# Normalising two attentions after the value product instead of before it, in a fused two-block transformer kernel

## The reference

```python
def causal_block_attention(q, k, v):          # 8 heads, q and k 96 wide, v 64 wide
    sc = jnp.einsum('bhqd,bhkd->bhqk', qi, kf) * scale
    sc = jnp.where(key_idx[None, :] <= q_idx[:, None], sc, -jnp.inf)
    p = jax.nn.softmax(sc, axis=-1)
    return jnp.einsum('bhqk,bhkd->bqhd', p, vf)
...
h = h + jnp.concatenate([o_gla, o_mla], axis=-1) @ w_out      # gated linear attention, then the above
hn = rms_norm_2(h, norm_xa)
xq = rms_norm_2((hn @ xa_w_q).reshape(b, s, 4, 128), xa_q_norm)
p = jax.nn.softmax(xq . xk * 128 ** -0.5)                     # cross attention, 4 heads of 128, 256 keys
h = h + (p @ xv).reshape(b, s, 512) @ xa_w_o
```

## Time and profile before

| | |
|---|---|
| executions | 971.32, 969.14, 969.3 us, median 969.3 |
| the profiled execution | 971.32 us, span of its records 969.6 us |
| PE / PEld busy | 960.1 us (99%) / 943.8 us (97%) |
| DVE / ACT / POOL busy | 689.9 us (71%) / 535.2 us (55%) / 123.3 us (13%) |
| chain that ended last | PE 96%, DVE 2%, DMA 1%, ACT 1% |
| granted PE clock | full in all 40 slices |

### The profile page before, as it was taken

How to read it: one execution, slowest core, us unless ns; L and a number is a source line. 1 busy time by engine, 2 the same in 40 slices (tenths; PEclk the granted TensorE clock), 3 DMA queues, 4 the chain that set the end, 5 groups by cost and what they waited for, 6 DMA issues and landing times.

```text
span 969.6 us, 20487 instructions
## 1 busy us (share of the span) xinstructions
PE 960.1 (99%) x8286; PEld 943.8 (97%) x8286; DVE 689.9 (71%) x1081; ACT 535.2 (55%) x775; POOL 123.3 (13%) x81
## 2 busy tenths in 40 slices
PE   7999999999999999999999999999999999999998
PEld 7999999999999999999999999989999999999998
DVE  4766766467869968877767655687697688788752
ACT  6545455345658964465544465477565665455531
POOL 0211110000026100002111102300001022223100
PEclk9999999999999999999999999999999999999999
DMA  7776575555454454575666674245245355665761
GB/s 245 217 214 204 185 239 180 182 152 185 150 199 153 135 170 135 173 258 178 209 187 206 206 233 154 88 143 173 87 140 172 125 174 163 193 207 173 251 208 63
DMA packets 169086, 172.37 MB, mean 178 GB/s; under 512 B 5684, under 2 KB 166974, under 8 KB 168894
## 3 DMA queue, kind: packets, MB, share of 16 engines
q1 hardware_dynamic: 169006, 171.45, 55.5%
q10 hardware_dynamic: 16, 0.00, 0.0%
HBM read 170.39 MB, written 1.06 MB: 177 GB/s over the span
## 4 chain that ended last, share of the span: by engine, by line
PE 96%; DVE 2%; DMA 1%; ACT 1%; issue 0%; SPq 0%; DVEq 0%
PE acc L730 86%; PE part L776 1%; PE acc L776 1%; DMA xraw<-in_x 1%; PE part L816 1%; PE part L840 1%; DVE wl L474 1%; PE part L1124 1%; PE part L826 1%; DVE al L1906 0%; PE part L860 0%; PE part L1114 0%; PE part L1320 0%; PE part L1301 0%; PE part L1147 0%; PE part L939 0%
## 5 line engine op out<-in xcount | busy, mean ns | idle before, releaser
L455 ACT ACTIVATE wh<-raw 128x1024 fp32r<-128x1024 f32 (+2 forms) x292 | 317.2, 1111 | 270.5 <-PE acc L730 122.7
L474 DVE TENSOR_TENSOR wl<-raw,wh 128x1024 fp32r<-128x1024 f32 (+3 forms) x294 | 391.1, 1370 | 54.0 <-ACT wh L455 52.2
L730 PE MATMUL acc<-ah,wh 128*128 128x256 f32 x1520 | 424.7, 279 | 0.7 <-DVE al L1906 0.3
L730 PE MATMUL acc<-al,wh 128*128 128x256 f32 x1520 | 420.8, 277 | 0.0
L730 PE MATMUL acc<-ah,wl 128*128 128x256 f32 x1520 | 420.7, 277 | 0.0
L730 PEld LDWEIGHTS acc<-ah,wh 128*128 128x128 f32 x1520 | 285.3, 188 | 4.7 <-issue 3.6
L730 PEld LDWEIGHTS acc<-al,wh 128*128 128x128 f32 x1520 | 285.4, 188 | 0.1
L730 PEld LDWEIGHTS acc<-ah,wl 128*128 128x128 f32 x1520 | 285.4, 188 | 0.0
L2769 POOL TENSOR_TENSOR sil<-sil,rstd 128x512 f32<-128x512 f32 x33 | 61.5, 1863 | 307.6 <-ACT sil L1427 215.5
L730 PE MATMUL acc<-hh,wh 128*128 128x256 f32 x352 | 97.4, 277 | 0.0
L730 PE MATMUL acc<-hh,wl 128*128 128x256 f32 x352 | 97.3, 276 | 0.0
(11 more groups left out here) (444 smaller groups left out, 1525.6 us busy)
## 6 DMA issues: line engine op xcount, KB each, us to landing
raw<-in_ffn_w_up SPq DMA_DIRECT2D x33, 1024.0 KB, 5.3
raw<-in_ffn_w_down SPq DMA_DIRECT2D x24, 1408.0 KB, 6.3
raw<-in_w_in SPq DMA_DIRECT2D x33, 1024.0 KB, 5.3
raw<-in_ffn_w_gate SPq DMA_DIRECT2D x32, 1024.0 KB, 5.3
raw<-in_w_out SPq DMA_DIRECT2D x8, 1024.0 KB, 4.9
raw<-in_w_proj_attn SPq DMA_DIRECT2D x4, 1024.0 KB, 4.9
raw<-in_w_proj_mlstm SPq DMA_DIRECT2D x4, 1024.0 KB, 5.6
raw<-in_xa_w_kv SPq DMA_DIRECT2D x4, 1024.0 KB, 4.9
```

Of the source, the lines that this page charges most:

```text
L455: nc.scalar.activation(wh[:, slot, a * nw:b * nw], raw[:, slot, a * nw:b * nw], ACT.Copy).then_inc(S("w_hi"), 1)
L474: nc.vector.tensor_tensor(wl[:, slot, a * nw:b * nw], raw[:, slot, a * nw:b * nw], f(wh[:, slot, a * nw:b * nw]), SUB).then_inc(S("w_lo"), 1)
L730: ins = mm(dst, a, b, start=st and q == 0, stop=en_ and q == 2, skip_group_check=True)
```

## The change

The division by the row sum moves behind the value product in both attentions. `ml_divided` and `xa_divided` go, so the transposes wait for the exponentials. In `ml_outputs` and `xa_outputs` the operands change places: the transposed probabilities are the weights and the values move, 64 columns in the causal attention and 128 in the cross attention. The result is token by feature. DVE takes it out with a multiplication by the reciprocal of the sum into `ytok`, and four extra groups of four PE transposes (`lo_T` twice, `xo_T` twice) bring it back to feature by token. The first two slabs of `wo2` are multiplied in the order first half, transposes, first half of the next slab, second half, second half of the next, and steps of ACT and DVE are placed anew.

```diff
@@ PE
             def ml_transposes(u):
-                pe.wait_ge(*signal("ml_pn", u + 1))
+                pe.wait_ge(*signal("ml_ex", 4 * u + 4))
...
-                for pair in range(2):
+                for h in range(4):
+                    c = (4 * g + h) * 64
                     for b in range(blk + 1):
-                        for odd in range(2):
-                            h = 2 * pair + odd
-                            c = (4 * g + h) * 64
-                            ins = mm(Q[4][64 * odd:64 * odd + 64, pair * P:(pair + 1) * P], vm[:, b, c:c + 64],
-                                     probT2[:, b, h * P:(h + 1) * P], start=pair + b == 0, stop=b == blk, skip_group_check=True)
+                        ins = mm(Q[4][:, h * 64:(h + 1) * 64], probT2[:, b, h * P:(h + 1) * P], vm[:, b, c:c + 64],
+                                 start=h + b == 0, stop=b == blk, skip_group_check=True)
                 ins.then_inc(S("ml_pv"), 1)
...
             s, n = SLAB0["wo2"], ACC0["wo2"]
             open_acc(n)
-            product(s, 0, 8, n, ah, al, before=mixer_operand, narrow=(1, Q[0]))
+            product(s, 0, 8, n, ah, al, before=mixer_operand, part=0, used=(1, 1))
+            pe.wait_ge(*signal("ml_yo", 4))
+            pe.wait_ge(*signal("ml_pt", 4))
+            for j in (2, 3):
+                y_transposes(j, Q[j - 2], "lo_T")
             open_acc(n + 1)
-            product(s + 1, 0, 8, n + 1, ah, al)
+            product(s + 1, 0, 8, n + 1, ah, al, part=0, used=(0, 0), narrow=(1, Q[4]))
+            product(s, 0, 8, n, ah, al, before=mixer_operand, part=1, used=(1, 1))
+            product(s + 1, 0, 8, n + 1, ah, al, part=1, used=(0, 2))
...
-                pe.wait_ge(*signal("xa_pn", u + 1))
+                pe.wait_ge(*signal("xa_ex", 4 * u + 4))
...
-                        ins = mm(Q[pair][:, c * T + u * P:c * T + (u + 1) * P], xv[:, b, h * P:(h + 1) * P],
-                                 (probT2, probT3)[u][:, b, h * P:(h + 1) * P], start=u + c + b == 0, stop=b == 1, skip_group_check=True)
+                        ins = mm(Q[pair][:, u * 256 + c * P:u * 256 + (c + 1) * P], (probT2, probT3)[u][:, b, h * P:(h + 1) * P],
+                                 xv[:, b, h * P:(h + 1) * P], start=u + c + b == 0, stop=b == 1, skip_group_check=True)
...
+            def xo_transposes(pair):
+                pe.wait_ge(*signal("xa_yo", pair + 1))
+                for c in range(2):
+                    for b in range(TB):
+                        h, o = 2 * pair + c, (c * TB + b) * P
+                        ins = nc.tensor.transpose(Q[2 + pair][:, o:o + P], ytok[:, b, h * P:(h + 1) * P], ident)
+                ins.then_inc(S("xo_T"), 1)
...
-            product(s + 1, 0, 8, n + 1, mo, mlo, tokens=True, before=at((3, lambda: xa_transposes(0)), (4, lambda: xa_transposes(1)), (6, lambda: xa_outputs(0, 0)), (6, lambda: xa_outputs(1, 0))))
+            product(s + 1, 0, 8, n + 1, mo, mlo, tokens=True, before=at((0, lambda: xa_transposes(0)), (4, lambda: xa_transposes(1)), (6, lambda: xa_outputs(0, 0)), (6, lambda: xa_outputs(1, 0))))
+            xo_transposes(0)
+            xa_outputs(0, 1)
+            xa_outputs(1, 1)
...
                     if (part, k) == (0, 0):
-                        xa_outputs(0, 1)
-                        xa_outputs(1, 1)
+                        xo_transposes(1)
@@ ACT
-                    act.wait_ge(*signal("ml_yo", 2 * j - 2))
-                    ins = A_(ah[:, 2 * j:2 * j + 2, :], yl[:, j - 2, :, :], ACT.Copy)
+                    act.wait_ge(*signal("lo_T", j - 1))
+                    ins = A_(pairs(ah, j), Q[j - 2][:, :], ACT.Copy)
...
             split_hi(act, s)
+            ml_transposed(3)
             y_hi(0)
             y_hi(1)
-            ml_transposed(3)
-            y_hi(2)
-            y_hi(3)
             split_hi(act, s + 1)
             xk_squares(0)
             xk_squares(1)
+            y_hi(2)
+            y_hi(3)
...
-            split_hi(act, s + 4, only=0)
             xa_transposed(0)
...
+            split_hi(act, s + 4)
             xa_transposed(1)
-            split_hi(act, s + 4, only=1)
+            token_out("xv", 1, lambda b: xv[:, b, 256:512], ms7[:, 2:4])
             for j in range(2):
-                act.wait_ge(*signal("xa_pv", j + 1))
-                A_(pairs(mh, j), Q[j][:, :], ACT.Copy).then_inc(S("xo_hi"), 1)
+                act.wait_ge(*signal("xo_T", j + 1))
+                A_(pairs(mh, j), Q[2 + j][:, :], ACT.Copy).then_inc(S("xo_hi"), 1)
                 if j == 0:
-                    token_out("xv", 1, lambda b: xv[:, b, 256:512], ms7[:, 2:4])
                     split_hi(act, SLAB0["xo"] + 1)
@@ DVE
             def ml_leave(u):
+                dve.wait_ge(*signal("ml_ex", 4 * u + 4))
+                link(V.reciprocal(rin[:, u % 2, :], rsm[:, u % 2, :]))
                 dve.wait_ge(*signal("ml_pv", u + 1))
-                V.tensor_copy(yl[:, g, :, blk * P:(blk + 1) * P], two_t(Q[4][:, 0:256])).then_inc(S("ml_yo"), 1)
+                V.tensor_tensor(by_head(ytok[:, blk, 512 + 256 * g:768 + 256 * g], 4), by_head(Q[4][:, 0:256], 4),
+                                across(rin[:, u % 2, :], 64), MUL).then_inc(S("ml_yo"), 1)
...
             xk_out(1)
             ml_leave(3)
+            split_lo(dve, SLAB0["wo2"] + 1)
             y_lo(2)
             y_lo(3)
-            split_lo(dve, SLAB0["wo2"] + 1)
...
+            def xa_leave(pair):
+                if pair == 0:
+                    dve.wait_ge(*signal("xa_ex", 8))
+                    link(V.reciprocal(rin[:, :, :], rsm[:, :, :]))
+                dve.wait_ge(*signal("xa_pv", pair + 1))
+                for u in range(2):
+                    ins = V.tensor_tensor(by_head(ytok[:, u, pair * 256:(pair + 1) * 256], 2), by_head(Q[pair][:, u * 256:(u + 1) * 256], 2),
+                                          across(rin[:, u, 2 * pair:2 * pair + 2], P), MUL)
+                ins.then_inc(S("xa_yo"), 1)
...
+            xa_leave(0)
             xo_low(0)
             split_lo(dve, s + 1, only=0)
+            xa_leave(1)
+            split_lo(dve, s + 1, only=1)
             xo_low(1)
-            split_lo(dve, s + 1, only=1)
```

More of the change, by code:

```diff
@@ L96, in shared_signals @@
         "mixer2_pe": [("mem_ps", 4), ("kv_ps", 1), ("uk_ps", 3), ("gl_z", 1), ("uq_ps", 3), ("kq_T", 8),
-                      ("gl_keT", 1), ("gl_att", 1), ("gl_dS", 3), ("gl_o", 2), ("go_T", 2), ("xq_ss", 2)],
+                      ("gl_keT", 1), ("gl_att", 1), ("gl_dS", 3), ("gl_o", 2), ("go_T", 2), ("lo_T", 2), ("xq_ss", 2),
+                      ("xo_T", 2)],
     }
@@ L349, in build @@
         xtok = ytok
-        yl = xn[:, :, :].rearrange("p c t -> p (c t)").rearrange("p (g f) -> p g f", g=2)[:, :, 512:1024]\
-            .rearrange("p g (c t) -> p g c t", c=2)
         qsq = xn[:, :, :].rearrange("p (j c) t -> p j (c t)", c=2)
@@ L2507, in ml_maxima, with ml_leave @@
                                            op0=ADD, op1=MIN, accum_out=rmx[:, u % 2, h:h + 1]).then_inc(S("ml_mx"), 1)
-            def ml_divided(u):
-                w = (u % 2 + 1) * P
+            def ml_leave(u):
+                g, blk = u // 2, u % 2
                 dve.wait_ge(*signal("ml_ex", 4 * u + 4))
                 link(V.reciprocal(rin[:, u % 2, :], rsm[:, u % 2, :]))
[L2514 to L2520, removed]
                 dve.wait_ge(*signal("ml_pv", u + 1))
-                V.tensor_copy(yl[:, g, :, blk * P:(blk + 1) * P], two_t(Q[4][:, 0:256])).then_inc(S("ml_yo"), 1)
+                V.tensor_tensor(by_head(ytok[:, blk, 512 + 256 * g:768 + 256 * g], 4), by_head(Q[4][:, 0:256], 4),
+                                across(rin[:, u % 2, :], 64), MUL).then_inc(S("ml_yo"), 1)
             def gl_masks():
@@ L2606, in y_lo @@
                 else:
-                    ins = V.tensor_tensor(al[:, 2 * j:2 * j + 2, :], yl[:, j - 2, :, :], f(ah[:, 2 * j:2 * j + 2, :]), SUB)
+                    ins = V.tensor_tensor(pairs(al, j), Q[j - 2][:, :], f(pairs(ah, j)), SUB)
                 ins.then_inc(S("y_lo"), 1)
@@ L2616, in _ @@
             split_lo(dve, g0 + 3)
-            ml_divided(0)
             slab_used(dve, g0 + 2)
@@ L2623, in _ @@
             gl_masks()
-            ml_divided(1)
             split_lo(dve, g0 + 5)
@@ L2630, in _ @@
             gl_state(2)
-            ml_divided(2)
             split_lo(dve, SLAB0["xk"])
@@ L2638, in _ @@
             gl_gated()
-            ml_divided(3)
             xk_out(0)
@@ L2712, in _ @@
             xa_maxima(1)
-            xa_divided(0)
-            xa_divided(1)
             split_lo(dve, s + 4)
@@ L2719, in xo_low @@
                 dve.wait_ge(*signal("xo_hi", j + 1))
-                V.tensor_tensor(pairs(ml, j), Q[j][:, :], f(pairs(mh, j)), SUB).then_inc(S("xo_lo"), 1)
+                V.tensor_tensor(pairs(ml, j), Q[2 + j][:, :], f(pairs(mh, j)), SUB).then_inc(S("xo_lo"), 1)
             def xo_added(k):
@@ L2810, in _ @@
             norm_pairs("n6")
```

(2 more changed lines are left out.)

## The result

The changed kernel takes 975.3 us (median of 6, 973.31 to 976.08), the kernel before 969.28 us in the same comparison. The ratio is 1.0052, 95% interval 1.0042 to 1.0062. In a second comparison, where the kernel before had a median of 970.95 us, the same changed kernel took 975.28 us, ratio 1.0038 (1.0021 to 1.0055). These ratios lie near those of the means over all executions (17 of the changed kernel in the first comparison, whose median is 974.79); the ratios of the medians are 1.0062 and 1.0045. The forecast was 973.7 us, 1.0045 times the median before, slower with a chance of 0.84.

What follows compares the result with a forecast made beforehand. PE, busy 99%, bounds the kernel, so added PE steps cost full length. Terms 1.28 - 0.15 + 0.79 + 0.20 + 0.63 + 1.62 = +4.4 us on a median of 969.3 give 973.7 us; range 971.0 to 976.5.

Steps and rivals of the forecast that it cites:

- the value product: Causal attention: 48 calls with 128 weight columns at 0.101 us each, 4.86 instead of 3.58 us, so +1.28 us.
- the cross attention: From the `xo` transposes on: 0.8 us of transposes, 0.1 of fresh starts, 0.7 more waiting, together +1.62 us.
- the third slab: In `wo2`, PE waits for DVE's late addition that empties the accumulator, plus a fresh start: +0.63 us.
- Divisions: DVE multiplications and reciprocals leave the chains to the transposes; PE gains -0.15 us, DVE loses some 5 us net.
- `lo_T`: Eight added PE transposes that bring the causal attention's result back to feature by token: +0.79 us.
- pace: `wo2` products in the new block order: more at 0.118 us before the narrow matmul, 11.32 against 11.12, +0.20 us.
- The wait for `xv`: Before `xa_outputs(0, 1)` in the cross attention, PE waits for ACT to write `xv`: 0.7 us.
- the wait of 0.25 for `xa_leave(1)`: Cross attention: PE waits 0.25 us for DVE's second exit, which stands behind a half split in DVE's list.
- Covered waits: Rival: the new waits are covered and only PE work is added, +3.0 us, 972.3 us; chance 0.14.
- Longer waits: Rival: DVE steps late at the accumulator and in the cross attention, +6.5 us, 975.8 us; chance 0.13.
- Not slower: Rival: products take the faster pace, 64 moved columns cost 0.064 per record, no new waiting: -0.3 us, 969.0; chance 0.05.
- From the profile to the median: Whole execution: profiled 971.32 us gives 975.7; other two executions lie 2.1 lower, so 973.7 against their median of 969.3.

Runs made afterwards that it cites:

- swap_only: Kernel before with only the operands of the causal attention's value product exchanged, output not the reference's: ratio 1.0022, 958.36 us behind the first product.
- no_div: Kernel before without the 24 DVE multiplications that divide the probabilities in both attentions: ratio 0.9994, 956.71 us behind the first product.
- dve_order: Changed kernel with DVE adding the first `wo2` accumulator into `xT` ahead of the second half of the third slab's split: ratio 1.0038 to the kernel before.
- no_waits: Changed kernel with that addition ahead of the split's second half, and the second value product reading the first pair's `xv` columns: ratio 1.0031 to the kernel before.
- xa_order: Changed kernel with the cross attention's second value product moved behind the first half product of `xo`: 977.79 us, ratio 1.0069 to the kernel before.
- ml_only: Kernel before with only the causal attention's part of the change, the cross attention as before: ratio 1.0030 (1.0009 to 1.0051).
- after_again: Changed kernel, unedited, run again for a second profile: 975.28 us, 961.32 us behind the first product.
- xa_only: Kernel before with only the cross attention's part of the change: ratio 1.0010 (0.9992 to 1.0027).

## Why the prediction was right

The direction and the places held, and of the six terms of the sum all but the value product came within 0.2 us. Counted from the first product on, the sum of +4.4 stands against 4.1 measured. That it came so close is partly luck: the value product was put too low by 0.28, and the cross attention and the third slab too high by 0.16 and 0.07.

- **Value product, +1.28.** The mis-sized term: the units measured +1.56, 0.107 per record, not 0.101. I went by calls that move one column; the 64-column calls cost what 128-column calls do. 0.15 of it comes back in the score products behind three of the units, which take 0.05 less each. With the divisions this gives +1.2 for the stretch up to `wo2`, which measured +1.03; the rest lies in products between the units that went at a faster pace in the profile after (the 24 ahead of the third unit took 2.83 us, before 3.03 with the pause of 0.09), for a reason that is open. The estimate from the Trainium skill, "TensorE: Matmul & The Clock Gate", section "LDWEIGHTS (loading the stationary operand)", was +1.5, the closer one. The Trainium skill, "TensorEngine Tiling (Array Packing)", section "Performance Considerations", advises the form that the kernel before had, and `swap_only` agrees: 0.129 us per call in that form, 0.216 in the swapped one.
- **Divisions, -0.15.** Measured -0.1 to -0.2, by `no_div` and in the profile after, which has the same 3.27 us there. With what the exits add DVE lost 3.7 us, not 5, at no price.
- **`lo_T`, pace and the third slab, +0.79 + 0.20 + 0.63 = 1.62.** Measured 1.56. The transposes took 0.80. The wait is where it was put, for the reason given: `dve_order`, which moves the addition alone, makes the stretch 0.56 shorter.
- **Cross attention, +1.62.** Measured 1.46. The wait for `xv` was 0.6 instead of 0.7, and the wait of 0.25 for `xa_leave(1)` did not come, since DVE's half split began early enough. What the forecast did not see is that taking the wait for `xv` away would gain nothing, since waits for DVE come up in its place (`no_waits`).
- **Rivals.** Covered waits: both waits are there. Longer waits: no. Not slower: the products behind the first unit kept their pace (48 at 671.78 took 5.76 us, as before at 673.97), and `swap_only` shows that 64 moved columns are not cheap at 128 weight columns. The pace did change in single runs of products, in both directions; in `swap_only` the same 48 took 5.55.
- **From the profile to the median.** I subtracted 2.1 us from the profiled execution and did not ask where they lie. The second profile of before, an execution of 969.56 us, puts them into the opening: its first product is at 10.66 and not at 12.74. "Granted clock full" in the table of the profile before was no sign of a full pace there. The forecast of 973.7 is 4.4 above the median before; the medians moved by 6.0 in one comparison and 4.3 in the other, of which 4.1 are seen behind the first product. The forecast had no term for openings that differ between the kernels' executions, and came out 1.6 us below the first median.

## What to carry to other kernels

Where PE is busy 99% of the time, count a change in PE records first: moving a division from 24 probability tiles to their outputs took 3.7 us of DVE that cost nothing and added 16 transposes and dearer products on PE, which did. Values that are 64 wide were cheaper on the weight side, two heads side by side; with 128 weight columns to load, moving 64 columns instead of 128 earned nothing. And a wait that a profile shows need not be the binding one: take it away in an experiment, and look whether the stretch gets shorter or the next engine's wait grows.

## What the runs showed of the hardware

In one profile (`xa_order`) a wait of PE of 1.8 us in the middle of a busy stretch was followed by 4.4 us at a mean granted clock of 0.61, which took another 1.8 us; four of the six executions of that kernel have a mean granted clock of 1.000. The waits of 0.3 to 0.8 us were followed by no fall.

At the start the granted clock fell in three profiles, in which PE had waited for `x` 2.1 us in all with a longest wait of 1.9 (`dve_order`), 1.8 with 1.4 (`xa_order`) and 2.4 in one (`no_waits`). In three more PE went at the pace of the lower level until after its first product, with 1.00 in the clock column: the profile before (2.2 us of waits, longest 1.5), `ml_only` (1.1 and 0.7) and `swap_only` (1.6 in one). It went at the full pace behind 1.8 in one wait (`after_again`), 1.9 and 1.5 (`no_div`) and 1.6 in one (`xa_only`). The length of the wait alone doesn't tell these apart, and what does is open. Read the opening by the distance of PE's records, and not by the clock column alone.

And a step that uses the array in two halves of 64 columns is preceded by 0.09 us of pause which the same step on the whole array hasn't: 0.21 us from the last product to its start instead of 0.12.
